# A slot's filler quarters on VectorE and ScalarE placed ahead of the slot's evictions, in the second recurrence of a two-block model

## The reference

```python
def wkv_scan(r, v, decay, k, a_in, b_in, s0, reverse):
    def step(S, inp):
        rt, vt, wt, kt, at, bt = inp
        sa = jnp.einsum('bhij,bhj->bhi', S, at)
        S = S * wt[:, :, None, :] + sa[..., None] * bt[:, :, None, :] + vt[..., None] * kt[:, :, None, :]
        return S, jnp.einsum('bhij,bhj->bhi', S, rt)
...
y_rw = rwkv_readout(r_l, v_l, ys_l, dirs_l, rw_r_k, rw_lnx_g, rw_lnx_b)
b_na = y_na.astype(dt) * jax.nn.silu(keep(na_gate))
b_pool = y_pool.astype(dt) * jax.nn.silu(keep(pool_gate))
g_na, g_pool, g_rw = jnp.split(jax.nn.sigmoid(keep(merge_logits)), N_BRANCH, axis=-1)
merged = g_na * (b_na @ w_branch[0]) + g_pool * (b_pool @ w_branch[1]) + g_rw * (b_rw @ w_branch[2])
```

## Time and profile before

| what | us |
| --- | --- |
| median of 3 runs | 3463.37 |
| lowest and highest run | 3457.84, 3468.15 |
| the profiled execution: its time | 3464.82 |
| the profiled execution: its span in the trace | 3463.0 |
| the stretch of the recurrence and its filler in the span | 2476 to 3285 |

### The profile page before, as it was taken

One profiled execution on the slowest core, in us unless ns is written; L12 is line 12 of the kernel. 1 busy time (PEld: TensorE's weight loads), 2 busy tenths in 40 slices (PEclk: granted clock), 3 DMA queues, 4 the chain that ended last, 5 costly groups with the idle time before them and its releaser, 6 DMA issues.

```text
span 3463.0 us, 82764 instructions
## 1 busy us (share of the span) xinstructions
PE 3305.1 (95%) x37052; PEld 2997.5 (87%) x37052; DVE 2158.9 (62%) x3328; ACT 1564.7 (45%) x2410; POOL 179.9 (5%) x254
## 2 busy tenths in 40 slices
PE   8999999899889999999999999999899999999998
PEld 7988988899878888888889888988798989998987
DVE  8555755567557888885645544355566656656565
ACT  5433433445434444444434444333445545545433
POOL 0000000000000000000001010001211011110010
PEclk9999999999999999999999999999999999999999
DMA  5545544775435555555553333434433343333364
GB/s 204 206 168 180 212 169 175 271 253 174 169 127 181 184 191 185 184 189 202 191 183 125 118 143 128 148 131 151 157 131 121 115 136 120 133 127 125 114 232 150
DMA packets 94401, 571.59 MB, mean 165 GB/s; under 512 B 12688, under 2 KB 20912, under 8 KB 32096
## 3 DMA queue, kind: packets, MB, share of 16 engines
q1 hardware_dynamic: 80496, 511.85, 42.0%
q0 software_dynamic: 13552, 54.46, 4.6%
HBM read 535.98 MB, written 30.28 MB: 164 GB/s over the span
## 4 chain that ended last, share of the span: by engine, by line
PE 77%; DVE 9%; ACT 7%; issue 3%; DMA 3%; POOL 0%; SPq 0%; DVEq 0%; ACTq 0%; POOLq 0%
PE banks L292 15%; PE banks L293 7%; PE banks L1043 3%; PE banks L316 3%; PE banks L317 3%; PE banks L318 3%; PE banks L2170 3%; PE banks L1044 3%; PE banks L1045 3%; PE banks L279 3%; PE banks L280 3%; PE banks L281 3%; PE banks L2171 3%; PE banks L2172 3%; PE banks L2391 2%
## 5 line engine op out<-in xcount | busy, mean ns | idle before, releaser
L259 DVE TENSOR_TENSOR w_lo<-ring,w_hi 128x2048 fp32r<-128x2048 f32 x274 | 629.5, 2297 | 427.9 <-ACT w_hi L253 427.8
L253 ACT CAST w_hi<-ring 128x2048 fp32r<-128x2048 f32 x274 | 522.7, 1907 | 230.9 <-PE banks L281 94.8
L292 PE MATMUL banks<-x_two,w_hi 128*128 128x512 f32 x1408 | 497.7, 399 | 0.0
L293 PE MATMUL banks<-x_two,w_lo 128*128 128x256 f32 x1408 | 395.4, 281 | 0.0
L1043 PE MATMUL banks<-x_two,w_hi 128*128 128x256 f32 x1152 | 345.0, 299 | 5.1 <-DVE w_lo L1110 5.1
L2226 DVE TENSOR_TENSOR w_lo<-ring,w_hi 128x512 fp32r<-128x512 f32 x316 | 208.6, 687 | 198.5 <-ACT w_hi L2183 197.1
L1044 PE MATMUL banks<-x_two,w_hi 128*128 128x256 f32 x1152 | 328.7, 285 | 0.0
L1045 PE MATMUL banks<-x_two,w_lo 128*128 128x256 f32 x1152 | 328.3, 285 | 0.0
L292 PEld LDWEIGHTS banks<-x_two,w_hi 128*128 128x128 f32 x1408 | 264.6, 188 | 66.1
L2170 PE MATMUL banks<-XK,w_hi 128*128 128x256 f32 x1024 | 304.8, 298 | 0.0
L2171 PE MATMUL banks<-XK,w_hi 128*128 128x256 f32 x1024 | 289.9, 283 | 0.0
(11 more groups left out here) (570 smaller groups left out, 7762.9 us busy)
## 6 DMA issues: line engine op xcount, KB each, us to landing
ring<-in_w_up SPq DMA_DIRECT2D x88, 1024.0 KB, 4.8
ring<-in_w_dil SPq DMA_DIRECT2D x72, 1024.0 KB, 5.0
mod_ring<-in_w_mod SPq DMA_DIRECT2D x48, 1024.0 KB, 8.1
ring<-in_w_logit SPq DMA_DIRECT2D x48, 1024.0 KB, 5.0
ring<-in_w_down SPq DMA_DIRECT2D x44, 1024.0 KB, 4.8
ring<-in_w_delta SPq DMA_DIRECT2D x32, 1024.0 KB, 4.8
ring<-in_w_out SPq DMA_DIRECT2D x32, 1024.0 KB, 4.8
ring<-in_w_na SPq DMA_DIRECT2D x32, 1024.0 KB, 4.8
```

What stands on the lines that cost most here:

```text
L253: nc.scalar.copy(w_hi[:, s, 0:w], ring[:, s, 0:w]).then_inc(S("panel_hi"), 4)
L259: nc.vector.tensor_tensor(w_lo[:, s, 0:w], ring[:, s, 0:w], w_hi[:, s, 0:w].bitcast(F32), ALU.subtract).then_inc(S("panel_split"), 4)
L292: nc.tensor.matmul(out_ap, hi, both, start=first_, stop=False)
L293: return nc.tensor.matmul(out_ap[:, 0, :], lo, both[:, 0, :], start=False, stop=last_)
```

## The change

In `rw_act` and `rw_dve` the call `F(turns(i, slot))` is moved from behind the evictions of its slot to ahead of them. Places where one quarter stood between two evictions are merged into the call of the next slot. `rw_pe`, the number of quarters per slot, the semaphores and the evictions themselves stay as they are.

```diff
@@ rw_act
             back, back2 = inv and tau == 0 and it_ > 0, inv and tau == 1 and it_ > 0
+            F(turns(i, "A"))
             if inv:
                 act.wait_ge(S("rw_mm"), mm("n", b))
...
             if back2:
                 roots(it_ - 1)
-            F(turns(i, "A"))
+            F(turns(i, "B"))
             if st:
                 solution(s_, 0)
...
-            F(turns(i, "B"))
             F(turns(i, "C"))
+            F(turns(i, "D"))
             if st:
                 right_side(s_, 1)
...
-            F(turns(i, "D"))
+            F(turns(i, "E"))
             if st:
                 solution(s_, 1)
...
-            F(turns(i, "E"))
             F(turns(i, "F"))
+            F(turns(i, "G"))
             if inv:
                 turned(b, 1)
-            F(turns(i, "G"))
+            F(turns(i, "H"))
...
             if nx:
                 exps(b + 1)
-            F(turns(i, "H"))
+            F(turns(i, "I"))
             turned(b, 2)
-            F(1)
             if back:
                 squares(it_ - 1)
-            F(turns(i, "I") - 1)
             F(turns(i, "J"))
@@ rw_dve (slots A to F in the same way)
                 last.then_inc(S("rw_dve"), 1)
                 vv.here("yacc", s_)
-            F(1)
             if nx:
                 cumulate(b + 1)
-            F(turns(i, "G") - 1)
+            F(turns(i, "H"))
...
-            F(turns(i, "H"))
+            F(turns(i, "I"))
             masked(b, 2)
...
-            F(1)
             if nx:
                 b_tilde(b + 1)
                 keys(b + 1)
                 if (b + 1) % 4 >= 2:
                     key_sums(b + 1)
-            F(turns(i, "I") - 1)
+            F(turns(i, "J"))
             if nx:
                 k_tilde(b + 1)
                 a_tilde(b + 1)
             joined(b, 2)
...
-            F(turns(i, "J"))
```

More of the change, by code:

```diff
@@ L2947, in rw_dve @@
                 inverse_root(it_ - 1, 1)
-            F(turns(i, "B"))
+            F(turns(i, "C"))
             if st:
@@ L2959, in rw_dve @@
                 affine(it_ - 1)
-            F(turns(i, "C"))
+            F(turns(i, "D"))
             if inv:
@@ L2973, in rw_dve @@
                 rates(b + 1)
-            F(turns(i, "E"))
+            F(turns(i, "F"))
             if st and s_ % 4 < 3:
@@ L2984, in rw_dve @@
                 lows(it_ - 1)
-            F(turns(i, "F"))
+            F(turns(i, "G"))
             if inv:
```

## The result

The changed kernel takes 3489.02 us (median of 4 runs, 3483.04 to 3495.03), the kernel before 3460.61 (4 runs, 3453.82 to 3468.15). The ratio is 1.0084, 95% interval 1.0068 to 1.0101: 28 us slower. The profiled execution took 3488.3 us.

The account below looks back on a forecast made before the run. TensorE was taken to bound the kernel, busy 95% of the span, with only its waits for evictions affected. Terms 36.6 - 3.9 = 32.7 us on the profiled 3464.8 gave 3497.5, by the median 3496; range 3478 to 3512.

Parts of the forecast that it names:

- the six loops: Loops 4 to 6 and 10 to 12, where fourth positions are second quarters: 36.6 us more waiting by PE.
- The signs: Checks named beforehand: new PE waits in loops 4 to 6 and 10 to 12, other loops within 2 us.
- f + 1.7: In slot F of loop 5, `GL` starts 1.7 us after f, PE's start on its quarters; forecast to stay.
- The second-quarter terms: Per-slot PE waits for evictions queued behind a fourth position that is a pair's second quarter: together 36.6 us.
- C: Slot C: `advance`, `iX`, `iT` end at f + 5.5 against 3.4, 2.2 us in three loops, sum 6.6.
- I: Slot I: gate work and table load delay `masked` and `turned`; less about 3.0 regained at `XF`, sum 3.9 us.
- H: Slot H: `joined` 1.0 us late, and `TK`, `exps`, quarters, `masked`, `turned` end at f + 10.8; sum 3.9 us.
- The clock: Rival: short PE waits lower TensorE's granted clock, some 25 us on top, 3516 us; chance 0.12.
- What changes sign: Loops 0, 2, 7, 8, 9, 13, 14: table load and branch evictions change place, net gain 3.9 us.
- B, D, H and J terms: Waits in these four slots; up to half, put at 12.5 us, would go if later shorter waits made up lateness.
- No change: Rival: the shift only changes places with existing waits; sum within 10 us, 3463 to 3473 us; chance 0.07.
- faster: Rival: fourth positions are seldom what is late, so only gains remain, about 8 us, 3455 us; chance 0.04.

Follow-up runs that it names:

- e9: Changed kernel with VectorE's slot I quarters moved back behind `masked` and AR: 3459.27 us, ratio 1.0001 to the kernel before.
- e3: Kernel before with only ScalarE's list (`rw_act`) changed, VectorE's list as before: 3434.28 us, ratio 0.9920 to the kernel before.
- e8: Kernel before with one ScalarE call moved: slot H's quarters ahead of the TK copy and `exps`: 3433.46 us, ratio 0.9907.
- e1: Changed kernel with two quarters in every slot of loops 1 to 14, so no second-quarter fourth positions: 3447.69 us, ratio 0.9951 to the kernel before.
- e4: Changed kernel, but fourth positions that are second quarters of a pair issued behind the slot's evictions: 3450.42 us, ratio 0.9964 to the kernel before.
- e6: Changed kernel with turns making fourth positions the second quarter of their pair in loops 2 to 15: 3550.47 us, ratio 1.0243 to the kernel before.
- e7: Kernel before with only ScalarE's list changed, and turns that leave no second-quarter fourth positions: 3424.6 us, ratio 0.9890 to the kernel before.

## Why the prediction was right, and where it was off

The forecast was 3496 us, 32.7 us slower; measured were 28. The direction, the range and the mechanism held, but part of the closeness is luck, since three errors cancel: the waits of the six loops were put 10.2 us too high, their busy time, which grew by 12.4, was left out, and the gain in the other loops was put 5.6 us too low. Together this makes 29.2 us in loops 0 to 14 out of a sum of 32.7.

**The signs.** The six loops grew by 4.9, 8.4 and 4.0 us (I had 5 to 6 each) and by 8.4, 5.9 and 7.2 (6 to 8). All the new waits that I had named appeared, `GL` in slot F of loop 5 still starts at f + 1.7, and PE waits nowhere for `w_lo`. Two of the other loops moved by more than the 2 us that I allowed: loop 2 became 3.2 us shorter and loop 7 2.4.

**The second-quarter terms** were right in kind and place, and each was too large. The growth of PE's waits in the six loops, by the slot that causes them, from the timelines:

| slot | my sum | measured | single waits after |
| --- | --- | --- | --- |
| F | 3.6 | 3.3 | 1.67 twice |
| G | 4.8 | 4.5 | 1.49 three times |
| E | 1.3 | 0.7 | 0.41, none, 0.31 |
| A | 3.9 | 2.8 | 0.52 and 0.40, three times |
| C | 6.6 | 4.5 | 1.16, 0.94, 1.16 for the state, 0.42 three times for `iT` |
| I | 3.9 | 1.8 | 1.61, 1.90, 1.68, less 3.4 that `XF` is waited for less |
| B | 3.4 | 2.6 | 0.83, 0.90, 0.83 |
| D | 2.1 | 0.9 | 0.16 three times, and 0.40 for `turned` in loop 6 |
| H | 3.9 | 2.2 | 0.87, 1.28, 0.87 for `joined`; those for `iBC` 4.8 instead of 5.6 |
| J | 3.1 | 2.7 | 2.24, 2.24, 1.83 instead of none, 1.01, 2.57 |

With 0.4 us of small waits this is the 26.4 us by which the idle time of PE grew (from the windows: 11.8 in loops 4 to 6, 14.6 in loops 10 to 12), where I had 36.6. C and I were each 2.1 us too large, H 1.7.

**The clock** was not in the sum; I had it as a rival with a chance of 0.12 that would give 3516. It came in part: five slow stretches, 8.5 us, about a third of the rival's 25. With the 3.9 us of busy time that the clock does not explain, the six loops' 38.7 us come out near my 36.6, by a sum that held only waits.

**What changes sign** was too small. The loops outside of the six became 9.5 us shorter, where I had 3.9. Loop 2 gave 3.2 us instead of 1.6. In loop 13 the branch eviction ahead of `XF`, for which I had added 1.3, is not felt (the wait for `XF` is 1.06 us, 0.99 before). Loop 0 grew by 0.9 instead of 1.9, since its wait for `XF`, 1.47 us before, is gone. Loops 7 and 9 gave 4.4 instead of 3.0, and 1.7 of that is a slow stretch in loop 7 before that is not there after.

**The range** has a slip. The text takes off "up to half" of the B, D, H and J terms and puts 12.5 us for it, which is the whole of them; half is 6.3. The lower end would be 3487 with it. The measured 3489 lies inside either way.

**Where my reasoning was blind.** I costed the run from `exps` to `turned` in slots H and I with the quarters on it as if they had to be there. The rows showed VectorE idle for a `w_hi` that ScalarE had queued behind `exps`, and I took that for the nature of the run and not for a matter of the order. So I saw neither that the change keeps this coupling (e9: worth 29 us) nor that moving one of the two engines alone dissolves it (e3, e8). The sentences that mislead are "Between two evictions both engines still have two quarters nearly everywhere; they are those of the next slot instead of the last one. So the work per slot is the same, and two things differ". There is a third: which slot's quarters they are on one engine, relative to the other. The forecast did not suffer by it, since the coupling costs nearly the same before and after.

**The rivals.** "No change" and "faster" are refuted for this kernel. The faster rival's idea, that only gains remain if the fourth positions do not bind, is what e1 and e4 show once they are put elsewhere. Both gain more than its 8 us.

What stays open: why the granted clock falls after some waits and not after others. The changed kernel has a low slice behind a 2.24 us wait at the start of loop 5 and none behind an equal wait at the start of loop 6, and one behind a wait of 1.84; the earlier trace rows has one at a 2.6 us wait. No run here varied the waits one by one. Also open is the part of the added busy time that the clock does not explain.

For e8 and e9 the windows of loops 0 to 14 tell where the time went. In e8 they are 21.6 us shorter than before, 21.4 of it idle time of PE. In e9 they are 24.9 us shorter than in the changed kernel, 17.0 of it idle and 8.0 busy time. The 29 us of the medians hold a few us more in both; the profiled executions themselves differ by 24.6 and 27.2 us, and part of that lies ahead of loop 0, where nothing was changed.

## What to carry to other kernels

When work is run ahead of evictions on several in-order engines, look at each wait inside that work, not at its busy time: a buffer that only comes free during the same slot turns "ahead" into "behind the consumer", and all evictions behind it are late. Look also at pairs of engines: if one hands work to the other, being one slot ahead on the producer alone can be worth more than being ahead on both. Here one moved call on ScalarE won 29 us, while moving both lists lost 28, and won 15 once no fourth position was a second quarter (e1).

## What the runs showed of the hardware

Many waits of up to 2.3 us between bursts of matmuls cost more than themselves. In e6 and e7 PE does nearly the same matmuls in loops 1 to 14; these are their windows, e6 first:

```profile
2513.20:3315.68 802.48, 709.71 (x15289) 669.23 (x15289) 456.60 (x816) 403.04 (x744) 80.17 (x115) 0.98 0.34 114
...
2507.10:3196.77 689.67, 684.75 (x15301) 652.53 (x15300) 456.56 (x819) 405.12 (x745) 81.26 (x116) 1.00 0.39 132
```

PE is idle for 92.8 us in e6, in waits of at most 2.3 us each, and for 4.9 in e7. It is busy for 25 us more in e6. The granted clock of 0.98 over 802 us is worth some 16 us of this, an estimate from the first row; what the other 9 are, no run here shows.
